# Gated up-projections: all products of a block's upper weights first, then all of the lower ones

## What is computed

```python
def swiglu(h, wg, wu, wd):
    return (jax.nn.silu(h @ wg) * (h @ wu)) @ wd

def second_block(x, ...):
    for i in range(DEPTH_2):          # 2
        x = x + 0.5 * swiglu(rmsnorm_2(x, ffn_norm1[i]), ffn1_wg[i], ffn1_wu[i], ffn1_wd[i])
        ...                           # attention
        x = x + 0.5 * swiglu(rmsnorm_2(x, ffn_norm2[i]), ffn2_wg[i], ffn2_wu[i], ffn2_wd[i])
    return x
```

## Time and profile before

| | us |
|---|---|
| median of 3 runs | 1272.0 (1271.95 to 1272.06) |
| the profiled execution | 1280.09 |
| its span, first to last instruction | 1278.4 |
| TensorE busy in it | 1236.0 (97%), 7068 products |
| VectorE busy | 880.3 (69%) |
| ScalarE busy | 613.1 (48%) |
| products of L289 and L291 | 1408 each |
| mean granted TensorE clock | 0.995 of full speed |

### The profile page before, as it was taken

How to read it: one execution, slowest core, us unless ns; L and a number is a source line. 1 busy time by engine, 2 the same in 40 slices (tenths; PEclk the granted TensorE clock), 3 DMA queues, 4 the chain that set the end, 5 groups by cost and what they waited for, 6 DMA issues and landing times.

```text
span 1278.4 us, 17927 instructions
## 1 busy us (share of the span) xinstructions
PE 1236.0 (97%) x7068; PEld 1062.2 (83%) x7068; DVE 880.3 (69%) x1077; ACT 613.1 (48%) x789; POOL 154.3 (12%) x164
## 2 busy tenths in 40 slices
PE   7999999999799999979999999999999899999998
PEld 7987899998688888867888888888888777888887
DVE  5975665556677766675976676867766675876675
ACT  6665534333544444575544344443444684544332
POOL 4420401202400000250100000100000430100000
PEclk9999999999899999999999999999999999999999
DMA  9882369777675555452565565655653312565530
GB/s 313 249 242 74 115 169 201 216 169 162 220 247 179 192 197 180 153 158 86 179 198 182 182 195 165 203 181 183 195 183 118 132 61 101 172 195 191 180 122 33
DMA packets 163369, 219.62 MB, mean 172 GB/s; under 512 B 13692, under 2 KB 141760, under 8 KB 163180
## 3 DMA queue, kind: packets, MB, share of 16 engines
q1 hardware_dynamic: 153324, 212.28, 52.5%
q0 software_dynamic: 9984, 6.49, 3.1%
HBM read 213.26 MB, written 5.25 MB: 171 GB/s over the span
## 4 chain that ended last, share of the span: by engine, by line
PE 81%; DMA 8%; DVE 5%; ACT 3%; issue 1%; POOL 0%; SPq 0%; DVEq 0%; ACTq 0%; POOLq 0%
PE ps L289 26%; PE ps L291 13%; PE ps L261 12%; PE ps L263 12%; PE ps L262 12%; DMA raw<-in_w_ff 5%; DMA raw<-in_ffn_wu 3%; PE ps L603 1%; DVE w_lo L237 1%; ACT w_hi L230 1%; PE ps L628 1%; PE ps L616 1%; DVE arena L708 1%; PE ps L428 1%; PE ps L257 1%
## 5 line engine op out<-in xcount | busy, mean ns | idle before, releaser
L230 ACT CAST w_hi<-raw 128x2048 fp32r<-128x2048 f32 (+3 forms) x198 | 373.8, 1891 | 446.5 <-PE ps L291 277.0
L237 DVE TENSOR_TENSOR w_lo<-raw,w_hi 128x2048 fp32r<-128x2048 f32 (+3 forms) x195 | 445.1, 2284 | 174.6 <-ACT w_hi L230 173.7
L289 PE MATMUL ps<-h_both,w_hi 128*128 128x512 f32 x1408 | 498.8, 398 | 1.0 <-DVE h_both L492 1.0
L291 PE MATMUL ps<-h_both,w_lo 128*128 128x256 f32 x1408 | 394.6, 280 | 0.0
L289 PEld LDWEIGHTS ps<-h_both,w_hi 128*128 128x128 f32 x1408 | 264.4, 188 | 67.7 <-issue 2.4
L291 PEld LDWEIGHTS ps<-h_both,w_lo 128*128 128x128 f32 x1408 | 265.7, 189 | 1.4
L261 PE MATMUL ps<-w_hi,act_hi 128*128 128x512 f32 x480 | 188.4, 393 | 1.4 <-DVE act_lo L1104 1.4
L263 PE MATMUL ps<-w_hi,act_lo 128*128 128x512 f32 x480 | 187.5, 391 | 0.0
L262 PE MATMUL ps<-w_lo,act_hi 128*128 128x512 f32 x480 | 187.1, 390 | 0.0
L296 DVE TENSOR_REDUCE arena<-ps 128x512 f32<-128x1024 f32 x88 | 107.7, 1224 | 82.5 <-PE ps L291 82.0
L367 POOL TENSOR_SCALAR rstd<-sums 128x1 f32<-128x1 f32 (+1 forms) x24 | 25.6, 1065 | 734.7 <-ACT scratch L356 659.2
(11 more groups left out here) (246 smaller groups left out, 1321.5 us busy)
## 6 DMA issues: line engine op xcount, KB each, us to landing
raw<-in_ffn_wg SPq DMA_DIRECT2D x44, 1024.0 KB, 5.3
raw<-in_ffn_wu SPq DMA_DIRECT2D x44, 1024.0 KB, 5.3
raw<-in_ffn_wd SPq DMA_DIRECT2D x44, 1024.0 KB, 4.9
raw<-in_w_ff SPq DMA_DIRECT2D x32, 1024.0 KB, 18.9
raw<-in_a_w_in SPq DMA_DIRECT2D x5, 1024.0 KB, 5.4
raw<-in_w_in SPq DMA_DIRECT2D x4, 1024.0 KB, 7.5
raw<-in_w_out SPq DMA_DIRECT2D x4, 1024.0 KB, 6.5
raw<-in_a_w_out SPq DMA_DIRECT2D x4, 1024.0 KB, 4.9
```

The source lines that it names most:

```text
L230: nc.scalar.copy(w_hi[:, place(b), 0:n], raw[:, b % RAW, 0:n]).then_inc(hi_ready, 1)
L237: nc.vector.tensor_tensor(w_lo[:, place(b), 0:n], raw[:, b % RAW, 0:n], w_hi[:, place(b), 0:n].bitcast(F32), ALU.subtract).then_inc(lo_rea ...
L289: nc.tensor.matmul(ps[:, bank + f, :], hi[:, k, f * P:(f + 1) * P], h_both[:, k, :, :].rearrange("p a b -> p (a b)"), start=k == 0, stop=F ...
L291: last = nc.tensor.matmul(ps[:, bank + f, 0:TOK], lo[:, k, f * P:(f + 1) * P], h_both[:, k, 0, :], start=False, stop=k == KD - 1, skip_gro ...
```

## The change

For every block but the one with `wait_h`, the 16 long products of the upper weights are issued first (both halves `f`), and then the 16 short ones of the lower weights. The block waits for `hi_ready` ahead of its first product, and for `lo_ready` only ahead of the first short one. For the gate block of step 0 the first half `f` stays in pairs; its second half is eight long products, then eight short ones. The number of products, their operands and the banks stay the same; 21 blocks of each stage have one wait more (84 in all, some of them in a loop's body). Nothing on the other engines or queues is changed.

```diff
         def wide_features_out(b, bank, turn=0, wait_h=None):
 
-            nc.tensor.wait_ge(lo_ready, b + 1 + RAW * turn)
+
             hi, lo = parts(b)
-            for f in range(2):
+
+            def of_hi(f, k):
+                nc.tensor.matmul(ps[:, bank + f, :], hi[:, k, f * P:(f + 1) * P], h_both[:, k, :, :].rearrange("p a b -> p (a b)"),
+                                 start=k == 0, stop=False, skip_group_check=True)
+
+            def of_lo(f, k):
+                return nc.tensor.matmul(ps[:, bank + f, 0:TOK], lo[:, k, f * P:(f + 1) * P], h_both[:, k, 0, :],
+                                        start=False, stop=k == KD - 1, skip_group_check=True)
+
+            if wait_h is not None:
+                nc.tensor.wait_ge(lo_ready, b + 1 + RAW * turn)
                 for k in range(KD):
-                    if wait_h is not None and f == 0 and k % 2 == 0:
+                    if k % 2 == 0:
                         nc.tensor.wait_ge(h_lo_ready, wait_h + k // 2 + 1)
-                    nc.tensor.matmul(ps[:, bank + f, :], hi[:, k, f * P:(f + 1) * P], h_both[:, k, :, :].rearrange("p a b -> p (a b)"),
-                                     start=k == 0, stop=False, skip_group_check=True)
-                    last = nc.tensor.matmul(ps[:, bank + f, 0:TOK], lo[:, k, f * P:(f + 1) * P], h_both[:, k, 0, :],
-                                            start=False, stop=k == KD - 1, skip_group_check=True)
+                    of_hi(0, k)
+                    of_lo(0, k)
+            else:
+                nc.tensor.wait_ge(hi_ready, b + 1 + RAW * turn)
+                for k in range(KD):
+                    of_hi(0, k)
+            for k in range(KD):
+                of_hi(1, k)
+            if wait_h is None:
+                nc.tensor.wait_ge(lo_ready, b + 1 + RAW * turn)
+                for k in range(KD):
+                    of_lo(0, k)
+            for k in range(KD):
+                last = of_lo(1, k)
             last.then_inc(block_used, 1)
```

## The result

The changed kernel takes 1265.4 us (median of 4 runs, 1264.3 to 1267.1) against 1272.0: a ratio of 0.9948 with a 95% interval of 0.9935 to 0.996. Measured again with 7 runs it is 1264.9 against 1271.85, ratio 0.9939 (0.9918 to 0.996). So it is faster by about 0.55%, as forecast (1264.5).

The account below looks back on a forecast made before the run. TensorE's product distances were taken to bound the gated stages; 36 steps at 0.213 us less give -7.7, first steps +0.25, so 1272.0 - 7.5 = 1264.5 us. Forecast range 1263 to 1266; 8 in 10 range 1262.5 to 1272.8.

Parts of the forecast that it names:

- The bound: Gated stages: time is the sum of the distances between the starts of TensorE's products, and nothing else.
- The later wait gives nothing: Block starts: splits end 6.7 to 6.9 us ahead, so moving the wait gives zero; outer bound against 1.7 us.
- The new step: Steps 2 to 10 of four stages: gate 5.54, up 5.57, second product 5.47 us; 16.58 against 16.79.
- the slower rival: L289's long products stay at 238 ns in a run: 0.07 us more a block, +6.4 us, 1278.4 us; chance 0.07.
- stay cheap: Rival: short products keep 0.115 us while long ones fall to 226.7 ns: 6.8 us more gain, 1257.7; chance 0.02.
- The rule that the order could not matter: Product distance is columns over 2.4 plus about 2.5 ns, whatever the neighbour: 1272.0 us; small part of the first rival's chance.
- the sum: Whole kernel: -7.7 us from 36 steps plus 0.25 from first steps, -7.45 us.
- The first steps: Steps 0 and 1 of each stage, pairs already short: some 0.06 us more a stage, 0.25 us in all.
- The carry-over from the profiled execution: The 0.6% between profiled 1280.09 and median 1272.0 us carries over unchanged: 1272.0 - 7.5 = 1264.5 us.
- The first rival: Writing the profile brings the 352.5 ns rhythm; without the profiler order makes no difference: 1272 to 1272.9 us; chance 0.23.
- only after a stage's first second product: Gated stages: pairs take 346.7 ns in step 1 and become 352.5 ns after the stage's first `second_product`.

Follow-up runs that it names:

- second profile of before: The kernel before the change, no edit, profiled once more: 1272.3 us for this execution, span 1270.5.
- changed kernel again: The changed kernel measured once more, no edit, against the kernel before: ratio 0.9939 (0.9918 to 0.996), 1263.7 to 1267.1 us.
- the order alone: Changed kernel's new order of products, but each block waits for its split in front, as before: 1264.5 us, ratio 0.9942 against the kernel before.
- the waits alone: Kernel before with its pairs kept; only the wait on the split moves behind the first long product: 1272.3 us, ratio 1.0001.

## Why the prediction was right, point by point

**The bound** held: in the gated stages the time is the sum of the starts' distances on TensorE. **The later wait gives nothing** is shown by the two halves of the change taken apart: 1.0001 for the waits, 0.9942 for the order.

**The new step** was put at 5.54 + 5.57 + 5.47 = 16.58 us and is 16.57. The bound on long products of L289 in a run was 226.7 to 238 ns; they stand at 226.7 from the sixth or seventh on, as F0's, and the slower rival falls with that (it needed a mean over 233.4). The short ones take 1.91 us for 16, as in F0, so they don't stay cheap either. The rule that the order could not matter falls as well: by the Trainium skill (TensorE: Matmul & The Clock Gate, section Back-to-back issue gap) the distance is the columns over 2.4 plus about 2.5 ns. The page gives this for a product by itself, and says of a stream with weight loads that loads and products set the distance together, so the prediction's "whatever the neighbour" read more into it than it states. The runs show 226.7 and 120.0 ns, the columns over 2.4 plus 13.3, in runs of one width, and other distances beside a product of another width. That it is the width, and not the change from upper to lower operands, F0 and the second products show: their products of one width go through upper and lower parts in turn (`product`) and stand at 120.0 and 226.7 ns all the same. Over 36 steps the gain is 36 x 0.220 = 7.9 us, where the sum had 7.7.

**The first steps** were put at +0.25 us. From the two traces taken side by side (second profile of before, changed kernel again), the three blocks after step 0's gate block go from 16.727 to 16.791 us in F1 and take 0.265 more over the four stages, which is the term. What it left out is step 0's gate block: 5.892 to 5.852 us in F1, 0.066 less over the four stages, so +0.20 in all. The pairs of that block's second half were in the slow rhythm in F1 to F3 (232, 118, 240, 120, 236), and there grouping them gained 0.02 to 0.04 us; in F4 they were quick (230, 117), and it gained nothing.

**The carry-over from the profiled execution** is the one step whose reason was wrong, though the number stood. The span fell by 13.0 us, not 7.5. Of these 8.1 lie before F1 (the late load) and 7.7 are the gated products' (7.9 less the 0.2 of the first steps); MA took 93.6 us in place of 90.1 because of the clock, and MB 0.7 less, where the first profile of before had the lower clock level for 3.4 us and that of after had not. The sum was made of distances, so neither touched it, and the median was right to start from. **The first rival**, that the profiler brings the slow rhythm, had drawn its chance from these 8.1 us, and falls: a second profile of before has the same steps of 16.79 us in 1272.3 us. Had I looked for the 8 us in the trace, the wait of 7.25 us before L428 would have shown them.

**The missing 0.7 to 1.0 us.** The gated steps give 7.7 us and the medians 6.7 and 7.0. The granted clock explains it. The execution of the changed kernel at 1267.1 us had the lower level for 3.4 and 6.8 us within MA (from 554 and 564 us on), the one at 1263.7 had none there. Busy time by stretch, 30 us of MA, after, then the same of the changed kernel again:

```profile
550.00:580.00 30.00, 25.25 (x158) 16.20 (x160) 20.43 (x97) 24.61 (x93) 10.39 (x18) 0.83 0.21 61
```

```profile
550.00:580.00 30.00, 24.55 (x176) 16.59 (x176) 23.34 (x105) 26.02 (x97) 10.42 (x18) 1.00 0.22 65
```

With the clock at 0.83, 158 products start in place of 176; MA takes 93.56 us against 90.12. TensorE has short idle times there (1.4 to 1.6 us at most, behind VectorE and ScalarE). Both profiles of before had none of these dips in MA.

The executions without a trace have their mean granted clock on record, and it splits them. In the traces it is 0.998 or more without a dip in MA and 0.996 or less with one (the first profile of before, with its late load, has 0.995 too). In the comparison of "The changed kernel again" 15 of 20 executions of before have 0.999 or 1.0, with a median of 1271.8 us, and 4 of 7 of the changed kernel, with a median of 1264.0: 7.8 us apart, beside the steps' 7.7. So the missing part fits the share of executions with a dip. Whether the change makes them more frequent is not shown: the changed kernel and the order alone have 8 of 18 at 0.997 or less, the old order (before and the waits alone) 15 of 46, and so few don't tell the two apart.

**What stays open.** Why pairs have two rhythms is not settled: a slow one of 352.8 to 353.3 ns a pair (repeating after three pairs) and a quick one of 346.5 to 346.8 (231, 112, 233, 117, or 230, 117). In every trace with the old pairs the blocks right behind a run of 24 equal products, long or short, are slow, even with small products between. Pairs hand on the rhythm they are in. Small products behind slow pairs end the slow rhythm (19 of 19 in step 0), and behind idle time or the short waits of step 0's gate block either can come. The prediction's "only after a stage's first second product" was the right place, and the cause named there, a rhythm into which the engine falls behind it, has been confirmed by putting such a run elsewhere. What in the engine does it no run here shows.

## What to carry to other kernels

Where TensorE is never idle, sum the distances between starts for each kind of product and compare them with the same kind in another order elsewhere in the same trace: here runs of equal widths cost 1.5 to 1.8% less a block than strict alternation in its slow rhythm, and the stage that already had such runs gave the price to 0.01 us. Against the quick rhythm they gain nothing (5.57 us a block against 5.55), so look first which one the pairs are in. Group products of equal width in long runs, and count each turn between such runs, from short to long and back, at about 0.02 us; between runs of two it is less (3 to 4 ns). Before a gap between the profiled execution and the median is used as an argument, look for the single wait that makes it.

## What the runs showed of the hardware that was not expected

- Alternating products of 512 and 256 columns have two stable rhythms, about 346.7 and 353 ns a pair, and a block keeps the one it has from its first pairs to its last: before, all 72 blocks of steps 2 to 10 take 5.64 or 5.65 us, and all 8 of step 1 take 5.55.
- Which rhythm comes depends on what ran in front: behind 24 equal products it is slow, even with four small products between; behind slow pairs the same four small products end it (19 of 19 blocks).
- The first long products behind short ones are dearer by 27 ns in all (233, 236, 228, 233, 230 against 226.7), behind only two short ones by 10 (232, 231).
- An idle stretch of 4.4 us in front of each of 40 gate blocks costs more than itself: the lower clock level behind it adds 2.55 us to the block in the mean (8.19 against 5.64), so the kernel grew by 284 us for 178 us of waits (40 x 2.55 = 102 us make the rest but for 4).
